# Expert weights of a mixture-of-experts layer: three 2 MB transfers per block in place of six of 1 MB

## The reference, cut to what matters

```python
def expert_block(args):
    xblk, e = args                                        # 128 rows x 1024
    gate, up = jnp.split(xblk @ w13[e], 2, axis=-1)       # w13[e]: 1024 x 1024, 4 MB in float32
    return (jax.nn.silu(gate) * up) @ w2[e]               # w2[e]: 512 x 1024, 2 MB in float32
```

## Time and profile before

| | |
|---|---|
| median of three runs | 2716.94 us |
| profiled execution, its own time | 2714.7 us |
| its span, first to last instruction | 2712.9 us |
| mean granted TensorE clock | 0.955 of full |
| busy: PE, DVE, ACT, GpSimd | 90%, 59%, 43%, 20% |
| DMA over the whole span | 397 MB, mean 146 GB/s |
| expert loop, about 2000 to 2615 us | 32 blocks |

### The profile page before, as it was taken

The page is one execution under the profiler, slowest core; times in us unless marked ns, Lnnn a source line. Parts: engine busy times, 40 slices in busy tenths (PEclk is TensorE's granted clock), DMA queues, the critical chain, the costliest instruction groups (busy, mean ns, idle before and its releaser), DMA issues.

```text
span 2712.9 us, 34477 instructions
## 1 busy us (share of the span) xinstructions
PE 2441.5 (90%) x13028; PEld 1997.9 (74%) x13028; DVE 1612.7 (59%) x2502; ACT 1174.7 (43%) x1480; POOL 545.8 (20%) x309
## 2 busy tenths in 40 slices
PE   6989999999999999999999999999579999999960
PEld 2289888888888889666999988855357777777750
DVE  3336988988988982000133321145758888888869
ACT  0324667667667675000000000000147777777751
POOL 0011221221221120000344411100013323232320
PEclk8979999999999999999999999999689999999985
DMA  7723233233233234111111131121359999999963
GB/s 270 270 58 83 59 103 93 59 101 95 59 94 98 63 89 156 56 46 48 40 47 46 46 102 41 29 89 59 121 211 343 342 350 346 351 356 341 340 211 141
DMA packets 255486, 396.98 MB, mean 146 GB/s; under 512 B 17572, under 2 KB 167724, under 8 KB 255322
## 3 DMA queue, kind: packets, MB, share of 16 engines
q1 hardware_dynamic: 232368, 344.63, 38.4%
q0 software_dynamic: 14080, 34.61, 3.4%
q10 hardware_dynamic: 8928, 16.26, 1.9%
HBM read 364.66 MB, written 48.22 MB: 152 GB/s over the span
## 4 chain that ended last, share of the span: by engine, by line
PE 59%; DVE 18%; ACT 9%; issue 8%; DMA 3%; SPq 1%; POOL 1%; DVEq 0%; ACTq 0%; POOLq 0%
PE bank L1901 8%; PE bank L1903 8%; PE bank L1902 8%; PE bank L2023 8%; PE bank L2117 5%; PE bank L2049 4%; ACT we_parts L1125 4%; DVE arena L1363 3%; PE bank L1847 2%; PE bank L2181 2%; PE bank L2184 2%; PE bank L2185 2%; DMA rows_dram<-arena 2%; DMA arena<-in_w_ada_dram 1%; DVE we_parts L1645 1%
## 5 line engine op out<-in xcount | busy, mean ns | idle before, releaser
L1901 PE MATMUL bank<-u_hi,w_pairs 128*128 128x344 f32 x1344 | 447.0, 333 | 9.1 <-DVE u_lo L1279 9.1
L1902 PE MATMUL bank<-u_lo,w_pairs 128*128 128x344 f32 x1344 | 431.5, 321 | 0.0
L1903 PE MATMUL bank<-u_hi,w_pairs 128*128 128x344 f32 x1344 | 431.4, 321 | 0.0
L1645 DVE TENSOR_TENSOR we_parts<-u_whole,we_parts 128x2048 fp32r<-128x2048 f32 x129 | 295.1, 2288 | 58.2 <-ACT we_parts L1125 58.1
L1125 ACT ACTIVATE we_parts<-u_whole 128x2048 fp32r<-128x2048 f32 x129 | 247.0, 1916 | 51.5 <-PE bank L2181 26.9
L1901 PEld LDWEIGHTS bank<-u_hi,w_pairs 128*128 128x128 f32 x1344 | 255.6, 190 | 14.0 <-DVE u_lo L1279 9.3
L755 POOL TENSOR_TENSOR w_pairs<-arena,w_pairs 128x1024 fp32r<-128x1024 f32 x56 | 150.9, 2695 | 545.1 <-ACT w_pairs L917 544.9
L1902 PEld LDWEIGHTS bank<-u_lo,w_pairs 128*128 128x128 f32 x1344 | 255.0, 190 | 3.9 <-issue 3.8
L1903 PEld LDWEIGHTS bank<-u_hi,w_pairs 128*128 128x128 f32 x1344 | 254.7, 190 | 0.0
L2023 PE MATMUL bank<-arena 128*128 128x344 f32 x768 | 222.2, 452 | 0.0
L2163 PE MATMUL bank<-we_parts,x_parts 128*128 128x512 f32 x512 | 210.2, 411 | 3.3 <-DVE we_parts L1645 1.8
(11 more groups left out here) (340 smaller groups left out, 5030.5 us busy)
## 6 DMA issues: line engine op xcount, KB each, us to landing
u_whole<-in_w_moe_dram SPq DMA_DIRECT2D x128, 1024.0 KB, 7.3
arena<-in_w_moe_dram SPq DMA_DIRECT2D x64, 1024.0 KB, 7.4
arena<-in_w_in_dram SPq DMA_DIRECT2D x88, 512.0 KB, 5.4
arena<-in_w_ada_dram SPq DMA_DIRECT2D x12, 2048.0 KB, 11.9
arena<-cum_dram ACTq DMA_DIRECT2D x62, 256.0 KB, 3.2
yb_dram<-arena POOLq DMA_DIRECT2D x8, 1032.0 KB, 4.9
arena<-in_state_ssm_dram SPq DMA_DIRECT2D x16, 512.0 KB, 5.8
out_dram<-arena SPq DMA_DIRECT2D x16, 512.0 KB, 4.9
```

Of the source, the lines that this page charges most:

```text
L1645: dve.tensor_tensor(w_los[v], wraw[slot], w_his[v].bitcast(F32), ALU.subtract).then_inc(wlo_ready, 1)
L1901: pe.matmul(out, hi[:, k, :], u_hi[:, k, at], start=(k == 0), stop=False)
L1902: pe.matmul(out, hi[:, k, :], u_lo[:, k, at], start=False, stop=False)
L1903: last = pe.matmul(out, lo[:, k, :], u_hi[:, k, at], start=False, stop=(k == KD - 1))
```

## The change

The two w2 slots become one stretch of `arena`, so that one transfer can fill both. The four w13 slots already lie side by side. One transfer now fills slots 0 and 3, one slots 4 and 5, one slots 1 and 2. Each waits until DVE has split the later of its two slots: after slot 2 for w2, after slot 3 for slots 0 and 3, after slot 5 for slots 4 and 5. ACT waits for the one semaphore of the pair (the second slot of a pair then finds it passed). Splitting, matmuls and all other instructions stay.

```diff
-        w2_raw = [r5.take(2 * D) for _ in range(2)]
-        wraw = [u_whole[:, 0:2 * D], *w2_raw] + [u_whole[:, 2 * D * x:2 * D * x + 2 * D] for x in range(1, 4)]
+        w2_raw = r5.take(4 * D)
+        wraw = [u_whole[:, 0:2 * D], w2_raw[:, 0:2 * D], w2_raw[:, 2 * D:4 * D]] + [u_whole[:, 2 * D * x:2 * D * x + 2 * D] for x in range(1, 4)]
...
-            def load_w13(j, x, expert):
-                sp.dma_start(wraw[j].rearrange("p (k c) -> p k c", k=2),
-                             w13_v[:, ds(expert * KD + 2 * x, 2), :]).then_inc(wraw_landed[j], 16)
+            def load_w13(x, expert):
+                at = 4 * D * x
+                sp.dma_start(u_whole[:, at:at + 4 * D].rearrange("p (k c) -> p k c", k=4),
+                             w13_v[:, ds(expert * KD + 4 * x, 4), :]).then_inc(wraw_landed[4 * x], 16)
...
+            def load_w2(expert):
+                sp.dma_start(w2_raw.rearrange("p (k c) -> p k c", k=4),
+                             w2_v[:, ds(expert * 4, 4), :]).then_inc(wraw_landed[1], 16)
...
-            for x, j in enumerate((0, 3, 4, 5)):
-                load_w13(j, x, 0)
             for x in range(2):
-                load_w2(x, 0)
-            for x, j in enumerate((0, 3, 4, 5)):
-                sp.wait_ge(wlo_ready, x + 1)
-                load_w13(j, x, 1)
+                load_w13(x, 0)
+            load_w2(0)
+            for x in range(2):
+                sp.wait_ge(wlo_ready, 2 * x + 2)
+                load_w13(x, 1)
...
-                    for j in range(6):
-                        sp.wait_ge(wlo_ready, i * 12 + (6 * b + 5 + j))
-                        if j in (1, 2):
-                            load_w2(j - 1, before)
-                        else:
-                            load_w13(j, max(j - 2, 0), expert)
+                    sp.wait_ge(wlo_ready, i * 12 + (6 * b + 7))
+                    load_w2(before)
+                    for x in range(2):
+                        sp.wait_ge(wlo_ready, i * 12 + (6 * b + 8 + 2 * x))
+                        load_w13(x, expert)
...
-            for x in range(2):
-                sp.wait_ge(wlo_ready, extra * 12 + (12 * PAIRS - 6 + x))
-                load_w2(x, expert)
+            sp.wait_ge(wlo_ready, extra * 12 + (12 * PAIRS - 5))
+            load_w2(expert)
...
-                act.wait_ge(wraw_landed[slot], n * 16 + (0 if slot in (1, 2) else 16))
+                act.wait_ge(wraw_landed[(0, 1, 1, 0, 4, 4)[slot]], n * 16 + (0 if slot in (1, 2) else 16))
```

More of the change, by code:

```diff
@@ L655, in _ @@
                 load_x0(i)
-            def load_w13(j, x, expert):
-                sp.dma_start(wraw[j].rearrange("p (k c) -> p k c", k=2),
-                             w13_v[:, ds(expert * KD + 2 * x, 2), :]).then_inc(wraw_landed[j], 16)
-            def load_w2(x, expert):
-                sp.dma_start(wraw[1 + x].rearrange("p (k c) -> p k c", k=2),
-                             w2_v[:, ds(expert * 4 + 2 * x, 2), :]).then_inc(wraw_landed[1 + x], 16)
+            def load_w13(x, expert):
[5 more added lines that the diff above has]
+                             w2_v[:, ds(expert * 4, 4), :]).then_inc(wraw_landed[1], 16)
             sp.wait_ge(wo_done, TILES + 1)
             sp.wait_ge(u2_ready, TILES + 1)
-            for x, j in enumerate((0, 3, 4, 5)):
-                load_w13(j, x, 0)
             for x in range(2):
-                load_w2(x, 0)
-            for x, j in enumerate((0, 3, 4, 5)):
-                sp.wait_ge(wlo_ready, x + 1)
-                load_w13(j, x, 1)
+                load_w13(x, 0)
[3 more added lines that the diff above has]
+                load_w13(x, 1)
             sp.wait_ge(routed, 1)
@@ L684, in _ @@
                 for b in range(2):
-                    n = i * 2 + (b + 2)
                     before, expert = expert_of(i * 2 + (b + 1)), expert_of(i * 2 + (b + 2))
-                    for j in range(6):
-                        sp.wait_ge(wlo_ready, i * 12 + (6 * b + 5 + j))
-                        if j in (1, 2):
-                            load_w2(j - 1, before)
-                        else:
-                            load_w13(j, max(j - 2, 0), expert)
+                    sp.wait_ge(wlo_ready, i * 12 + (6 * b + 7))
[3 more added lines that the diff above has]
+                        load_w13(x, expert)
             expert = expert_of(extra * 2 + (2 * PAIRS - 1))
```

## The result

The median went from 2718.44 us (four runs, 2716.14 to 2720.68) to 2893.72 us (four runs, 2891.40 to 2895.27): slower, ratio 1.065, 95% interval 1.0636 to 1.0663. The profiled execution's span grew from 2712.9 to 2889.7 us, + 176.8. All of it lies in the expert loop: ACT starts the slots of block 1 at 1998.61 us, 0.95 us earlier than before (1999.56), and the first longer period is the next one, as forecast. There are thirty longer periods: ACT starts slot 0 of block 31 at 2767.43 us, where it was 2589.10.

A forecast was written before the change was run, and what follows sets the result against it. The prediction took a ring of ACT, DVE and PE as the bound. 12.55 + 0.17 + 12.7 + 0.3 + 0.1 gave a 25.8 us period against 19.7; 30 x 6.1 = + 183 us, forecast 2900 us, range 2830 to 2965.

The forecast's parts named there:

- The place of the new wait: ACT's split of slot 0 waits for the pair of slots 0 and 3, some 6 us in each of 30 blocks.
- Steps 1 to 3: From a block's first weight pass on ACT (T) to pass 2's end on DVE: T + 12.55 us.
- step 2: DVE's pass 1 no longer waits for ACT, held by token-row transposes: 0.39 us goes, T + 12.64 to T + 12.25.
- step 3: PE's clock falls after idling, slowing transposes in the chain to pass 2: 0.3 us taken, to T + 12.55.
- Step 4: SP issues w2 0.17 us after pass 2 ends, at T + 12.72.
- Steps 5 and 6: Queue: pair lands 12.7 us after w2's issue, gather adds 0.3, ACT starts 0.1 after the landing.
- The sum: Expert loop: new block period 25.8 us against 19.7, + 6.1 us, times 30 makes + 183 us.
- In-order queue: Loads land one behind another, 2.6 us per further MB; rival that the pair does not queue behind w2: 2801, 8%.
- What else could be late: Slots 4 and 5 land at worst 5.2 us after the next T, w2 5.2 us ahead of the pair: neither late.
- PE as the bound: Rival: PE's clock stays low in the loop, 31.6 us of work per block, 3074 us; 8%.
- Faster through larger transfers: Rival: fewer, larger transfers relieve the DMA engines, PE's 18.2 us per block decides, 2672 us; 2%.
- the DMA share: Sign to look for in the loop: DMA engines' busy share near 0.75.

The follow-up runs named there:

- Experiment 1: Changed kernel, but slots 0 and 3 are 1 MB loads again, each issued when its own slot is split; 2718.02 us, ratio 1.0002.
- experiment 3: Changed kernel, but slots 0 and 3 are two 1 MB loads with own semaphores, both still issued after pass 3; 2811.72 us, ratio 1.035.
- experiment 6: Changed kernel with 18 unused matmuls more on PE at the head of each block but the first; 2886.02 us, ratio 1.0627.
- experiment 11: Changed kernel with gather and scatter of token rows held back until about 3.6 us after the coming block's pass 0 starts; 2893.3 us, ratio 1.0652.
- Experiment 4: Changed kernel, but w2's transfer is held back until pass 3 and issued behind that of slots 0 and 3; 2912.23 us, ratio 1.0711.
- experiment 5: Changed kernel, but all of w13 is one 4 MB transfer issued after pass 5; 3259.04 us, ratio 1.1993.
- Experiment 10: Kernel before with DVE's silu times up ahead of pass 1, and 2 MB transfers for w2 and for slots 4 and 5; 2701.86 us, ratio 0.9943.
- Experiment 7: Kernel before, loads unchanged, but DVE does silu times up ahead of its split of slot 1; 2693.0 us, ratio 0.991.

## Why the prediction came out right

- **The place of the new wait.** ACT's split of slot 0, once per block, for the load of u_whole, as forecast: in time 30 periods, in the rows 29 waits, and none for w2. Experiment 1 (no cost without this pair) and experiment 3 (95 us with late loads of 1 MB) show what does it: the late issue of slot 0 a little over half, the wait for both halves of the pair the other 82 us.
- **Steps 1 to 3**, pass 2 at T + 12.55. Measured T + 12.25 in the block shown and T + 12.39 in the one before it (2444.61 + 2.28 - 2434.50); the mean of 29 blocks is T + 12.36. With a full clock it is T + 11.91 (2467.16 + 2.28 - 2457.53 in experiment 6). So step 2 was too small, 0.73 goes from T + 12.64 and not 0.39, and so was step 3: the clock costs 0.3 to 0.5 there, 0.44 in the mean, against 0.3. In time it is 0.2 to 0.3 per block (experiment 6).
- **Step 4**: 0.18 us measured for 0.17.
- **Steps 5 and 6**, from w2's issue to the next pass 0: 12.7 + 0.3 + 0.1 = 13.1. Measured 13.12 and 13.18 (2485.80 - 2472.68; 2460.25 - 2447.07), 13.09 in the mean. The split of the sum was off: w2 takes 7.9 us where 7.5 was reckoned, and the gather, put at 0.3, costs the pair nothing that can be seen (experiment 11). That these two cancel is luck.
- **The sum**: 12.36 + 0.18 + 13.09 = 25.63 us against 25.8; + 5.9 us a block against + 6.1; + 177 us on the span against + 183. It is nearer than its terms are.
- **In-order queue.** Behind w2 the pair needs 9.6 to 11.0 us, w2 7.6 to 8.2. In the block shown w2 is there some 7.9 us after its issue, 2480.6, and the pair at 2485.70: 5.1 us, two times 2.6. Experiment 4 shows it the other way round.
- **What else could be late**: slots 4 and 5 land at T + 7.9 in the median and not by T + 5.2 or T + 6. The gather and the scatter cost them the difference (experiment 11), a price that the prediction looked for at the pair. w2 is issued at T + 12.5, so the queue is empty by then all the same, and ACT does not wait for them.
- **PE as the bound** did not come: the granted clock falls once per block and is back at 1.00 a few microseconds later, and PE is busy 80% of the stage. (The gap in the earlier trace rows that the prediction counts as a wait for a DMA was one for DVE; these here are for a load.) The stage table around the block shown, and the transposes, which fall into the slow stretch there, 1.01 us against 0.66:

```profile
2466.00:2468.00 2.00, 2.00 (x6) 1.15 (x5) 1.88 (x2) 0.73 (x1) 0.00 (x0) 0.50 0.43 172
2468.00:2469.00 1.00, 1.00 (x6) 0.98 (x6) 0.00 (x0) 0.02 (x1) 0.00 (x0) 0.65 0.00 0
2469.00:2470.00 1.00, 1.00 (x6) 0.82 (x5) 0.39 (x1) 0.58 (x1) 0.00 (x0) 1.00 0.00 0
```
```profile
2467.94 1.01 PE L2188 MATMUL bank<-arena 128*128 128x128 f32 x4
```

- **Faster through larger transfers** had no support in any run: 2 MB for w2 and slots 4 and 5 left the time as it was, 4 MB land like four times 1 MB.
- **Off**: the DMA share, 0.70 for some 0.75.

Some of the expectations behind the prediction failed on size. In experiment 4 pass 3 was placed 1 us too early: a longer wait for w2, and the half clock in the chain. In experiment 5 gather and scatter, issued with the start of the load, cost 2.8 us, where 0.7 was reckoned. They cost as much in the changed kernel, but there the transfer of slots 4 and 5 pays, for which nobody waits. Why two transfers of 0.27 MB cost 2.8 us stays open. Experiment 10 lost 9 us that its theory had not, and experiment 11's gain of 9 us didn't come.

## What to carry to other kernels

Group transfers by when their buffers come free and when they are needed, not by which addresses are neighbours: a group is issued when its last buffer is free and counts when its last byte has landed, and both ends fell here on the slot that the next block needs first (95 and 82 us). Before a batching, check that the queue has fixed costs to save (here queued 1 MB loads already followed each other in 2.6 us) and subtract: time from the last release to the first use, 4.6 us, against what is still ahead in the queue plus the transfer, 10.2 to 10.8 from the pair's issue. The difference is the 5.9 us. And where the waits name a ring of engines and not a load, the order on the engines is the place to look, even with the DMA engines busy 96% of the time; moving one DVE instruction gave 0.9% with the old loads.

## What was not expected of the hardware

- Two indirect transfers of 0.27 MB each cost a 4 MB load that starts with them 2.8 us (15.6 against 12.8). In the changed kernel they cost the transfer behind the pair about as much (T + 7.9 against T + 5.0), and the pair, which is further on when they are issued, nothing that can be seen.
- GpSimd's own instruction for an indirect transfer took 2.9 us in the kernel before and 1.0 in the one after. In experiment 11, where its two tiny additions run beside DVE's splits, those take 1.6 us for 0.2, and the indirect ones stay at 1.0. That suggests that DVE holds GpSimd up. Experiment 7, which changes the order on DVE alone, bears it out for one instruction: the scatter's, beside a split in the kernel before (2418.05, the split from 2417.73), takes 2.9 us there and 1.0 in experiment 7, where it starts in an idle stretch of DVE (2406.03, idle until 2406.67). What in DVE's split does it no run tells, and nothing waited for it. The loop's groups on GpSimd from 2100 to 2600 (busy us, mean ns): two of the kernel before, one of the kernel after, the scatter of experiment 7, and experiment 11:

```profile
L836 POOL DMA_INDIRECT arena<-u_dram,arena x26 | 75.7, 2913 | 13.3 <-issue 13.3
L840 POOL DMA_INDIRECT rows_dram<-arena x26 | 75.0, 2886 | 4.2 <-POOL arena L847 4.2
```
```profile
L833 POOL DMA_INDIRECT arena<-u_dram,arena x19 | 19.5, 1029 | 9.7 <-issue 9.7
```
```profile
L840 POOL DMA_INDIRECT rows_dram<-arena x27 | 27.5, 1019 | 4.4 <-POOL arena L847 4.2 <-issue 0.2
```
```profile
L844 POOL TENSOR_TENSOR arena<-arena 128x1 f32<-128x1 f32 x40 | 65.1, 1628 | 400.5 <-ACT x_parts L1127 400.0
L833 POOL DMA_INDIRECT arena<-u_dram,arena x20 | 20.7, 1034 | 2.9
```
